# Experts' gate/up weights in four transfers of half a matrix instead of two of a whole one

## The reference, cut to what matters

```
def expert_block(args):          # xb: the tokens of the block, e: its expert
    xb, e = args
    hid = jax.nn.silu(xb @ w1[e]) * (xb @ w3[e])     # w1, w3: 1024 x 256
    return hid @ w2[e]                               # w2: 256 x 1024
```

## Time and profile before

| what | value |
|---|---|
| median of three runs | 1515.65 us |
| profiled execution | 1517.73 us |
| its span on the core | 1516.0 us |
| mean granted TensorE clock | 0.966 |
| PE busy | 1421.8 us (94%) |
| PEld busy (weight loads, beside the matmuls) | 1070.9 us (71%) |
| DVE busy | 531.6 us (35%) |
| ACT busy | 523.4 us (35%) |
| POOL busy | 474.5 us (31%) |
| bytes moved by DMA | 286.51 MB, mean 189 GB/s |
| experts' gate/up and down transfers | 192 of 1024 KB |

### The profile page before, as it was taken

One profiled execution on the slowest core, in us unless ns is written; L12 is line 12 of the kernel. 1 busy time (PEld: TensorE's weight loads), 2 busy tenths in 40 slices (PEclk: granted clock), 3 DMA queues, 4 the chain that ended last, 5 costly groups with the idle time before them and its releaser, 6 DMA issues. The chain is left out here.

```text
span 1516.0 us, 27429 instructions
## 1 busy us (share of the span) xinstructions
PE 1421.8 (94%) x11430; PEld 1070.9 (71%) x11430; DVE 531.6 (35%) x1356; ACT 523.4 (35%) x1115; POOL 474.5 (31%) x455
## 2 busy tenths in 40 slices
PE   7999999989999999999899997959999999999985
PEld 6788876667888888888677885835666666666653
DVE  3103037742222101111406315163445445445435
ACT  4325447753322222222445432212222232222222
POOL 5334545534544444444437742400000000000000
PEclk9999999989999999999899998979999999999997
DMA  5223220113133223322233222553999999999994
GB/s 179 82 87 111 84 83 32 45 57 111 59 109 111 80 87 111 111 70 70 73 112 112 77 90 73 212 209 139 421 420 419 420 420 419 419 419 419 420 420 168
DMA packets 83740, 286.51 MB, mean 189 GB/s; under 512 B 8740, under 2 KB 31424, under 8 KB 59040
## 3 DMA queue, kind: packets, MB, share of 16 engines
q1 hardware_dynamic: 83232, 283.60, 48.2%
q0 software_dynamic: 288, 1.05, 0.2%
q10 hardware_dynamic: 96, 0.08, 0.0%
HBM read 282.58 MB, written 2.13 MB: 188 GB/s over the span
## 5 line engine op out<-in xcount | busy, mean ns | idle before, releaser
L475 POOL TENSOR_TENSOR wring_halves<-wring,wring_halves 128x512 fp32r<-128x512 f32 x274 | 357.6, 1309 | 392.0 <-ACT wring_halves L470 391.3
L470 ACT CAST wring_halves<-wring 128x512 fp32r<-128x512 f32 x274 | 168.4, 621 | 442.5 <-PE ps L1084 426.8
L1082 PE MATMUL ps<-wring_halves,big_halves 128*128 128x512 f32 x612 | 241.5, 395 | 4.2 <-POOL wring_halves L475 2.7
L1082 PE MATMUL ps<-hT_halves,wring_halves 128*128 128x512 f32 x480 | 188.2, 392 | 1.7 <-DVE big_halves L1702 1.7
L2263 POOL TENSOR_TENSOR rstd<-rstd,half 128x1 f32<-128x1 f32 (+1 forms) x25 | 15.1, 606 | 554.4 <-DVE rstd L2216 514.4
L1083 PE MATMUL ps<-big_halves,wring_halves 128*128 128x512 f32 x480 | 187.5, 391 | 0.0
L1084 PE MATMUL ps<-hT_halves,wring_halves 128*128 128x512 f32 x480 | 187.4, 390 | 0.0
L1083 PE MATMUL ps<-wring_halves,hT_halves 128*128 128x512 f32 x436 | 171.0, 392 | 0.0
L1084 PE MATMUL ps<-wring_halves,hT_halves 128*128 128x512 f32 x436 | 170.7, 391 | 0.0
L1082 PEld LDWEIGHTS ps<-wring_halves,big_halves 128*128 128x128 f32 x612 | 115.5, 189 | 32.4 <-POOL wring_halves L475 5.3
L1509 PE MATMUL ps<-xn,fixed 128*128 128x512 f32 x256 | 122.7, 624 | 1.8 <-DVE fixed L2099 1.8
(11 more groups left out here) (332 smaller groups left out, 2079.0 us busy)
## 6 DMA issues: line engine op xcount, KB each, us to landing
big<-in_moe_w_dram SPq DMA_DIRECT2D x90, 1024.0 KB, 24.5
wring<-in_moe_w_dram SPq DMA_DIRECT2D x70, 1024.0 KB, 24.7
wring<-in_ffn_w_in_dram SPq DMA_DIRECT2D x22, 1024.0 KB, 6.7
hT<-in_moe_w_dram SPq DMA_DIRECT2D x20, 1024.0 KB, 25.4
wring<-in_fox_w_in_dram SPq DMA_DIRECT2D x7, 2048.0 KB, 8.4
wring<-in_gla_w_in_dram SPq DMA_DIRECT2D x6, 2048.0 KB, 8.2
mkv<-in_moe_w_dram SPq DMA_DIRECT2D x12, 1024.0 KB, 23.7
wring<-in_ffn_w_out_dram SPq DMA_DIRECT2D x4, 2048.0 KB, 7.8
```

The lines of the kernel that those rows point to most:

```text
L470: act.copy(hi, src).then_inc(s_hi, 1)
L475: pool.tensor_tensor(lo, src, hi, ALU.subtract).then_inc(s_lo, 1)
L1082: pe.matmul(out, lhs[1], rhs[0], start=start, stop=False)
```

## The change

`gate_up_in` issues four transfers for an expert instead of two: first the halves of `w1[e]` and `w3[e]` for parts `k` = 0 to 3 of the contraction, then those for `k` = 4 to 7. Each moves 512 KB, as 128 pieces of 4 KB (contiguous in SBUF's partition and in memory, with 8 KB from one piece to the next in memory). Each slot has two semaphores, one for each half. The product increments `s_gu` twice for each expert, after `k` = 3 and after `k` = 7. SP waits for the first increment of the slot's last user before the first two transfers and for the second before the other two. PE waits for the first half's transfers ahead of `k` = 0 and for the second's ahead of `k` = 4. ACT waits for the second increment. The loop for extra blocks waits for both halves. The down weights are as before.

```diff
-        s_e13 = [sem(f"expert_gate_up_in_{i}") for i in range(E_SLOTS)]
+        s_e13 = [[sem(f"expert_gate_up_in_{i}_{h}") for h in range(2)] for i in range(E_SLOTS)]
@@ gate_up_in, SP
                 w13 = w13_slot(j)
-                if last is not None:
-                    sp.wait_ge(s_gu, last)
-                for g, src in enumerate((W1, W3)):
-                    sp.dma_start(w13[:, g, :, :].rearrange("p k n -> p (k n)"), src[e]).then_inc(s_e13[j], 16)
+                half = KD // 2 * P * KF
+                for h in range(2):
+                    if last is not None:
+                        sp.wait_ge(s_gu, 2 * (last - 1) + h + 1)
+                    for g, src in enumerate((W1, W3)):
+                        sp.dma_start(w13[:, g, KD // 2 * h:KD // 2 * (h + 1), :].rearrange("p k n -> p (k n)"),
+                                     src[e][:, half * h:half * (h + 1)]).then_inc(s_e13[j][h], 16)
@@ silu, ACT
-                act.wait_ge(s_gu, b + 1)
+                act.wait_ge(s_gu, b * 2 + 2)
@@ gate_up, PE
-                last.then_inc(s_gu, 1)
+                    if k % (KD // 2) == KD // 2 - 1:
+                        last.then_inc(s_gu, 1)
@@ expert_in, PE
-                pe.wait_ge(s_e13[b % E_SLOTS], 32 * (b // E_SLOTS + 1))
                 wait(pe, s_mhid, b - 1)
-                gate_up(b, b % E_SLOTS, b % BUNCH, lambda i: pe.wait_ge(s_xT, 2 * (b // BUNCH) + i + 1))
+
+                def ready(i):
+                    pe.wait_ge(s_e13[b % E_SLOTS][i], 32 * (b // E_SLOTS + 1))
+                    pe.wait_ge(s_xT, 2 * (b // BUNCH) + i + 1)
+
+                gate_up(b, b % E_SLOTS, b % BUNCH, ready)
@@ the loop for extra blocks, PE
-                    pe.wait_ge(s_e13[0], i * 32 + 32 * (EXPERTS // E_SLOTS + 2))
+                    for h in range(2):
+                        pe.wait_ge(s_e13[0][h], i * 32 + 32 * (EXPERTS // E_SLOTS + 2))
```

## The result

The changed kernel takes 1525.82 us, a median of four runs (1525.28 to 1526.86), against 1515.58 us for the kernel before in the same session (1514.91 to 1516.1): a ratio of 1.0069, 95% interval 1.0051 to 1.0086. It is 10.2 us slower. In a later session it was 1524.74 against 1515.96, ratio 1.0060 (1.0046 to 1.0074), 8.8 us. The forecast was +5.3 us (1521.0, range 1516.5 to 1527.0). The direction and the mechanism of the main term were right, and the size was too small.

What follows compares the result with a forecast made beforehand. The prediction took the experts' DMA transfers, full from 1052 us, as the bound. Packets +6.2 us and earlier start -0.9 summed to +5.3, or 1523.0 on the profiled execution and 1521.0 for the median; range 1516.5 to 1527.

Steps and rivals of the forecast that it cites:

- the main term: Experts' stage: smaller gate/up packets on full DMA engines add boundaries for 57 experts, +6.2 us.
- h: Fixed DMA engine cost of each further packet, taken as 6 ns from trace values of 3.6, 6.8 and 9.2 ns.
- rival C: Experts' stage: 4 KB rows with 8 KB between them cost more than any earlier stream, +29.7 us, halfway +14; chance 0.11.
- The bound: Experts' stage: DMA transfers, full from 1052 us, set the end; TensorE's lead is used up by 1340.
- Part 1: Gate/up loads of experts 7 to 63: 16 more packet boundaries and 2 small packets per expert, +6.2 us.
- parts of 1 and 2: Two more small signal packets per expert, each at the fixed packet cost; five SyncE issues instead of three, costing nothing.
- Part 3: Gate/up slots: the first half is free some 1.0 us sooner, gain zero, bounds 0 and -1.0 us.
- Part 4: Last gate/up product, expert 63: starts on its first half, ending sooner after landing; gain 0.9 us, bounds 0 and 1.1.
- Part 5: TensorE: one more wait and a second increment per expert, cost nothing, 0.1 us at most.
- A: Experts' stage: packet boundaries are cheap and no difference shows, 1518.4 or 1514.8 us; chance 0.18.
- B: Experts' stage from 1340 us: slot release bounds, five laps each 1.0 us shorter, -5 us, 1510.7; chance 0.05.
- D: SyncE becomes the bound: five issues of 2.13 us make 10.7 us per expert, +180 us; chance 0.02.

Runs made afterwards that it cites:

- e2: Kernel before, with the slot laid out so each gate/up matrix stays one transfer but of 256 pieces of 4 KB: 1523.3 us against 1516.55, ratio 1.0052.
- e3: Kernel before, with each gate/up matrix still one transfer but of 512 pieces of 2 KB: 1539.08 us, ratio 1.0154.
- e9: Kernel before, with each gate/up matrix in two transfers, even and odd partitions, rows kept at 8 KB: 1515.43 us against 1515.71, ratio 0.9997.
- e4: Changed kernel, but SyncE waits for the whole product before both halves and TensorE for both halves before part 0: 1525.84 us, ratio 1.0064.
- e5: Kernel before, with only SyncE's order changed: gate/up one expert further ahead of down until expert 31: 1511.8 us against 1515.71, ratio 0.9973.
- e7: Kernel before, with four half transfers and the split wait for expert 63 alone: 1515.48 us against 1515.71, ratio 0.9998.
- e10: Kernel before, with four gate/up transfers per expert by even and odd partitions, each row in two 4 KB pieces, whole release and wait: 1523.38 us, ratio 1.0053.
- e12: Repeat of the kernel before with whole gate/up matrices in one transfer of 256 pieces of 4 KB: 1524.91 us, ratio 1.0055.
- e6: Changed kernel, with gate/up transfers issued one expert further ahead of down until expert 31: 1521.14 us, ratio 1.0032.

## Why the prediction was right, and where its size was off

The range held both medians, 1525.82 and 1524.74, and in part by its width. The forecast itself, with h from 3.9 to 9.2 ns, ended at 1524.1; both lie above it, in the part of the range that was lent from rival C.

**The bound.** Right. The transfers set the end: the full stretch grew with the number of packets (e2, e3), didn't move with the number of transfers (e9) or with the waits (e4), and moved with the start of the transfers (e5). TensorE's lead, which hid everything up to 1340, was used up sooner: it was busy 279.2 of 280 us from 1060 to 1340 and 277.9 in the changed kernel.

**Part 1, packets, +6.2 us.** The right mechanism, with h too small and the count a little too high: 6 ns taken, 8.3 to 8.8 measured where nothing is skipped in memory; 18 packets per expert taken, of which the two small ones cost nothing that shows (e9). With 8.5 ns and 16 packets, 57 x 16 x 8.5 = 7.8 us; the stretch of the changed kernel grew by 8.5 and 9.3, and the difference is the open rest. The two errors work against each other, and that of h is the larger one. The rows that I read gave 3.6, 6.8 and 9.2 ns, and I leaned to 3.6 since its rows were the longer. It came from two windows of one microsecond each in which 2 KB packets ran at 401 and 410 GB/s; held for 280 us, with down packets of 8 KB between them, kernel e3 has 397. Such a window is too short for what was asked of it: in the kernel before, slices of 2.5 us of the steady stage (1200 to 1300 us) scatter from 406 to 426 GB/s around 419, a spread of 15 ns for a packet of 8 KB and more than the whole h, and the burst of 2 KB rows was full for three microseconds. The spread of my three values was the honest sign, and its upper end the better choice. Of the two figures of the Trainium skill that stood beside it ("DMA: Bandwidth & Descriptors", "Why small descriptors are slow" and "iDMA fabric — 4 AXI ports for 8 engines, asymmetric across TPBs"), the estimate of 3.5 ns per packet is too low here, where 8.3 to 8.8 ns were measured, and the load stream with 4 KiB rows, by which it would be +7.5 us, comes close to the 7.6 of e2.

**The second small packet and the issues, parts of 1 and 2.** Two small packets per expert were put at h each, 0.7 us in all. e9 has them and shows 0.0 us, so their cost is below what can be seen. SyncE's issues cost nothing that shows, as forecast (e9). The backlog in time fell as said (25 to 16 forecast, 17.6 measured), and it did no harm.

**Part 3, earlier release, 0.** Right (e4).

**Part 4, earlier start, -0.9 us.** The term that was not reached, by its own condition "unless a transfer holds it". The last half product ends 1.1 us after its wait, as forecast, instead of 2.04. But the down product of 62 then stands idle for 1.14 us, where before it had none. It waits for its weights, which are behind in the same queue: they were issued at 1481.05 us and landed 18.3 us later, at 1499.4, and the product starts at 1499.46. I had checked the room for the last down transfer (63) and not for the one before it. In the kernel before, the weights of 62 were issued at 1463.93 and landed 26.6 us later, 0.7 us ahead of its product at 1491.18; no more than this could be gained. The tail is 27.8 to 28.0 us in the eight profiles of kernels whose last product ran in one piece, e4 apart (before, e2, e3, e5, e7, e9, e10, e12). In the first profile of the changed kernel it is 28.1 us; in its second and in e6 it is 27.3. There the weights of 62 landed 2.5 us after the last gate/up weights and not 3.3, and the down product waited less:

```profile
1498.20 1.07 PE L1571 MATMUL ps<-wring,arena 128*32 128x256 f32 x16 [0.26 <-issue]
```

So the early start gave 0.6 us in two profiles and nothing in one.

**Part 5, waits, 0.** Not tested by itself: e4 signals as often, and e2, e10 and e12, which have none of these waits, differ from the changed kernel by no more than the 0.5 to 1.7 us that are open.

Sum: +7.6 to +8.0 from packets, 0.5 to 1.7 us open, -0.6 to +0.2 from the tail. From the issue of the down transfer of expert 5 to the end of the span there are 464.0 us before and 472.7 and 472.6 in the changed kernel, 8.7 us more; the medians gave 10.2 and 8.8 in two sessions, and the forecast was 5.3. The profiled executions alone give 8.2 (1525.95 - 1517.73), since the first profile of before was one of its later ones, by where the stage began.

**The rivals.** A (nothing shows) falls by e2 and e3. B (laps) falls by e4, though the chain of waits linked the laps again and again; what ruled it out from the start was the share of 1.01 and the count of slots. C (costlier than any stream of before) falls in its size of +14 us, and where nothing is skipped in memory 8.8 ns is below the 9.2 of a row. The changed kernel itself, with 8 KB from piece to piece, has 8.5 to 9.3 us for 912 boundaries, 9.3 to 10.2 ns each, so a small part of C may be what is open. D (SyncE bound) falls by e9: the rate held at 419 with five issues.

## What to carry to other kernels

When the DMA engines are full over a stretch, count packets there and not transfers: halving the contiguous row costs a fixed time for each new packet, here 8 to 9 ns, and finer signalling pays only where someone waits for a part that has already landed. Halve a transfer by something that leaves its rows whole, and try how it is spread: by even and odd partitions it cost nothing here, by lower and upper 64 it took 350 us. And before making a full stretch finer, look at the moment where it starts: here a reordering of one queue, with no finer pieces, was worth 3.9 us.

## What the runs showed of the hardware that I had not expected

- With the gate/up transfers to 64 neighbouring partitions each, all 16 DMA engines are busy and the stage gets about half of the rate: 225 GB/s against 419, with 592 ns for a packet of 8 KB against 316. With 64 rows in even or in odd partitions it runs at 419 GB/s.
- How much waits in the sync queue is fixed neither in packets nor in bytes. Rate of packets times the issue-to-landing time gives, for one of 16 engines, 5733 / 1600 x 25.5 = 91 before, 6157 / 1600 x 21.8 = 84 in e9, 9374 / 1600 x 17.6 = 103 after, 8968 / 1600 x 20.7 = 116 in e2 and 15104 / 1600 x 15.8 = 149 in e3 (packets of the queue in 100 us). The bytes, in the same order, are 10.7, 9.1, 7.3, 8.5 and 6.3 MB. What sets the depth stays open.
- The stages before can shift the start of this one from execution to execution of the same kernel: 1049.90 and 1052.28 us in the two profiles of the kernel of e2, 1051.54 and 1050.39 in those of the changed one. The spans differ by about as much, 2.8 and 1.2 us, while a stretch inside the profile repeats to within a microsecond (436.0 and 435.9; 443.6, 443.8 and 444.0; 444.5 and 445.3).
